# Heads normalised and gated inside the tile loop of the second attention, and the modulation chunks split two, four and two around it

## Time and profile before

| | us |
|---|---|
| median of 3 runs (1449.39 to 1458.11) | 1451.26 |
| the profiled execution | 1451.47 |
| its span, first to last instruction | 1449.6 |
| PE busy | 1267.8 (87%) |
| DVE busy | 886.1 (61%) |
| ACT busy | 599.4 (41%) |

### The profile page before, as it was taken

The page is one execution under the profiler, slowest core; times in us unless marked ns, Lnnn a source line. Parts: engine busy times, 40 slices in busy tenths (PEclk is TensorE's granted clock), DMA queues, the critical chain, the costliest instruction groups (busy, mean ns, idle before and its releaser), DMA issues.

```text
span 1449.6 us, 18593 instructions
## 1 busy us (share of the span) xinstructions
PE 1267.8 (87%) x5990; PEld 861.6 (59%) x5990; DVE 886.1 (61%) x1354; ACT 599.4 (41%) x711; POOL 162.2 (11%) x184
## 2 busy tenths in 40 slices
PE   8899999896997988579679999999999999999910
PEld 1599999653352233154257777777777777777600
DVE  0621332245325721338358888888888888888888
ACT  1332222104003011210236766767767767667601
POOL 0100000000000200000001211211211112112102
PEclk9699999996975999859879999999999999999955
DMA  8232221504430860120499999999999999999896
GB/s 344 81 121 94 68 68 34 120 8 138 137 102 16 302 170 14 66 73 1 189 340 358 381 377 367 372 374 373 381 375 367 377 372 379 380 378 374 332 315 244
DMA packets 91519, 339.20 MB, mean 234 GB/s; under 512 B 12312, under 2 KB 35880, under 8 KB 65420
## 3 DMA queue, kind: packets, MB, share of 16 engines
q1 hardware_dynamic: 75104, 301.02, 57.8%
q0 software_dynamic: 16384, 37.78, 7.5%
HBM read 317.24 MB, written 42.48 MB: 248 GB/s over the span
## 4 chain that ended last, share of the span: by engine, by line
PE 82%; DVE 9%; DMA 4%; ACT 2%; issue 1%; SPq 1%; POOL 0%; DVEq 0%; POOLq 0%; ACTq 0%
PE ps L1556 13%; PE ps L1900 12%; PE ps L1884 8%; PE ps L1880 7%; PE ps L1881 6%; PE ps L1882 6%; PE ps L1769 5%; PE ps L1866 3%; PE ps L1587 3%; PE ps L1805 3%; PE ps L1504 2%; PE ps L1744 1%; PE ps L1833 1%; PE ps L1796 1%; DMA arena<-in_w_out 1%
## 5 line engine op out<-in xcount | busy, mean ns | idle before, releaser
L1403 DVE TENSOR_TENSOR gu_lo<-w_gu,gu_hi 128x1536 fp32r<-128x1536 f32 x128 | 224.4, 1754 | 2.3 <-ACT gu_hi L965 2.3
L965 ACT ACTIVATE gu_hi<-w_gu 128x1536 fp32r<-128x1536 f32 x128 | 189.8, 1483 | 0.1
L1398 DVE TENSOR_TENSOR down_lo<-arena,down_hi 128x2048 fp32r<-128x2048 f32 x64 | 146.7, 2293 | 33.9 <-ACT down_hi L971 33.3
L1880 PE MATMUL ps<-gu_hi,xT_hi 128*112 128x512 f32 x384 | 158.2, 412 | 3.0 <-issue 2.1
L1882 PE MATMUL ps<-gu_hi,xT_lo 128*112 128x512 f32 x384 | 152.3, 397 | 0.0
L1881 PE MATMUL ps<-gu_lo,xT_hi 128*112 128x512 f32 x384 | 152.3, 397 | 0.0
L1556 PE MATMUL ps<-w_hi,hT_hi 128*128 128x300 f32 (+1 forms) x480 | 145.2, 303 | 0.7 <-DVE w_lo L1037 0.7
L1556 PE MATMUL ps<-w_lo,hT_hi 128*128 128x300 f32 (+1 forms) x480 | 144.8, 302 | 0.0
L1556 PE MATMUL ps<-w_hi,hT_lo 128*128 128x300 f32 (+1 forms) x480 | 144.7, 301 | 0.0
L971 ACT ACTIVATE down_hi<-arena 128x2048 fp32r<-128x2048 f32 x64 | 121.9, 1904 | 0.0
L1884 PE MATMUL ps<-w_gu,arena 128*112 128x512 f32 x256 | 120.2, 591 | 0.0
(11 more groups left out here) (267 smaller groups left out, 1964.2 us busy)
## 6 DMA issues: line engine op xcount, KB each, us to landing
w_gu<-in_w_exp_gate SPq DMA_DIRECT2D x64, 1024.0 KB
w_gu<-in_w_exp_up SPq DMA_DIRECT2D x64, 1024.0 KB
arena<-in_w_exp_down SPq DMA_DIRECT2D x64, 1024.0 KB, 6.1
arena<-in_w_ada SPq DMA_DIRECT2D x24, 1024.0 KB, 5.6
arena<-in_w_in SPq DMA_DIRECT2D x12, 1200.0 KB, 5.7
arena<-expert_rows SPq DMA_DIRECT2D x9, 1024.0 KB, 12.6
arena<-expert_rows SPq DMA_DIRECT2D x4, 2048.0 KB, 12.7
arena<-in_x_prompt SPq DMA_DIRECT2D x8, 512.0 KB, 10.8
```

What stands on the lines that cost most here:

```text
L965: a.activation(gu_hi[b % RING][:, :, ks], w_gu[b % U][:, :, ks], ACT.Copy).then_inc(s_ghi, 1)
L1398: v.tensor_tensor(down_lo[:, :, :], w_dn[b % RING], down_hi[:, :, :].bitcast(F32), ALU.subtract).then_inc(s_dlo, 1)
L1403: v.tensor_tensor(gu_lo[b % U][:, :, ks], w_gu[b % U][:, :, ks], gu_hi[b % RING][:, :, ks].bitcast(F32), ALU.subtract).then_inc(s_glo, 1)
L1880: pe.matmul(out, x_hi, gu_hi[r][:, :, k], start=(k == 0), stop=False)
```

## The change

- PE: chunks 0 and 1 are multiplied whole in the gate stage, between the gate logits and the wait for the log gates; chunks 2 to 5 are laid in the loop's tiles 0 to 3; chunk 6 runs between the loop and the sample states, chunk 7 behind them. The waits on `s_goe` and `s_gkve` that stood between chunks 5 and 6 now stand behind chunk 7.
- The PSUM banks of the chunks change with it.
- ACT: the ten `silu` are moved ahead of the tile loop; the two squares of each tile are moved into the loop, behind the copy of its output.
- DVE: folds 0 and 1 behind the log gates; in tile t of the loop (t from 1) fold t+1, then the sum of the squares of tile t-1, and, behind the state additions (on tile 4 between the two `qm_g` products and the sample states), the seven passes of tile t-1. Behind the loop remain the squares' sum of tile 4, folds 6 and 7, and the seven passes of tile 4.
- SP: loads 1 to 13 instead of 1 to 10 ahead of the stores; behind them loads 14 and 15 instead of 11 to 15.

```diff
-        MOD2_BANK = (2, 2, 2, 2, 2, 3, 6, 7)
+        MOD2_BANK = (6, 7, 2, 2, 2, 2, 2, 3)
...
SP
-            for i in range(1, 11):
+            for i in range(1, 14):
                 load_mod2(i)
...
-            for i in range(11, 16):
+            for i in range(14, 16):
                 load_mod2(i)
...
ACT
             for t in range(NT):
                 R = ROWS[t]
+                step(a.activation(proj[0:R, t, C_RG:C_RG + RET_W], proj[0:R, t, C_RG:C_RG + RET_W], ACT.Silu))
+                a.activation(proj[0:R, t, C_GG:C_GG + RET_W], proj[0:R, t, C_GG:C_GG + RET_W], ACT.Silu).then_inc(s_ng, 1)
+            for t in range(NT):
+                R = ROWS[t]
                 for n in range(2):
                     a.wait_ge(s_gt, 2 * t + n + 1)
...
-            for t in range(NT):
-                R = ROWS[t]
-                step(a.activation(proj[0:R, t, C_RG:C_RG + RET_W], proj[0:R, t, C_RG:C_RG + RET_W], ACT.Silu))
-                a.activation(proj[0:R, t, C_GG:C_GG + RET_W], proj[0:R, t, C_GG:C_GG + RET_W], ACT.Silu).then_inc(s_ng, 1)
-            for t in range(NT):
-                R = ROWS[t]
                 a.wait_ge(s_nq, t + 1)
                 step(a.activation(proj[0:R, t, C_RK:C_RK + RET_W], proj[0:R, t, C_RQ:C_RQ + RET_W], ACT.Square))
+                a.wait_ge(s_goe, t + 1)
                 a.activation(proj[0:R, t, C_RV:C_RV + RET_W], proj[0:R, t, C_GO:C_GO + RET_W], ACT.Square).then_inc(s_sq, 1)
...
DVE
+            for n in range(2):
+                mod_fold(n)
...
+            def head_squares(t):
+                R = ROWS[t]
+                v.wait_ge(s_sq, t + 1)
+                mark(v.tensor_reduce(head_ss[0:R, t], ...), s_nv, t + 1)
+
+            def heads(t):
+                v.wait_ge(s_small, 16 * 7)
+                v.wait_ge(s_nr, t + 1)
+                v.wait_ge(s_ng, t + 1)
...
                 if t:
-                    mod_fold(t - 1)
+                    mod_fold(t + 1)
+                    head_squares(t - 1)
...
+                    if t:
+                        heads(t - 1)
                 else:
...
+                    heads(t - 1)
                     for h in range(H):
...
-            for n in range(4, 8):
+            head_squares(PT)
+            for n in range(6, 8):
                 mod_fold(n)
+            heads(PT)
...
PE
+            for n in range(2):
+                mod_mm(n)
             pe.wait_ge(s_ls, 2)
...
                 if t < PT:
-                    pe.wait_ge(s_fold, 2 + t)
-                    mod_part(t, 0)
+                    pe.wait_ge(s_fold, 4 + t)
+                    mod_part(2 + t, 0)
...
-                        mod_part(t, 1 + c)
-                    mod_part(t, 3)
+                        mod_part(2 + t, 1 + c)
+                    mod_part(2 + t, 3)
...
+            pe.wait_ge(s_fold, 2 + 6)
+            mod_mm(6)
             for h in range(H):
...
-            pe.wait_ge(s_fold, 2 + 4)
-            mod_mm(4)
-            mod_mm(5)
+            mod_mm(7)
             pe.wait_ge(s_goe, NT)
             pe.wait_ge(s_gkve, 2 * H)
-            mod_mm(6)
-            mod_mm(7)
```

More of the change, by code:

```diff
@@ L1176, in _ @@
                 mark(v.tensor_tensor(k, k, ex[0:R, t % 2, 1], ALU.mult), s_gm, t + 1)
+            def head_squares(t):
+                R = ROWS[t]
+                v.wait_ge(s_sq, t + 1)
+                mark(v.tensor_reduce(head_ss[0:R, t], proj[0:R, t, C_RK:C_RK + 2 * RET_W].rearrange("p (h v) -> p h v", h=2 * H), AX.X, ALU.add), s_nv, t + 1)
+            def heads(t):
+                R = ROWS[t]
+                v.wait_ge(s_small, 16 * 7)
+                v.wait_ge(s_nr, t + 1)
+                v.wait_ge(s_ng, t + 1)
+                for n, (at, gate) in enumerate(((C_RQ, C_RG), (C_GO, C_GG))):
+                    o = proj[0:R, t, at:at + RET_W]
+                    o3 = o.rearrange("p (h v) -> p h v", h=H)
+                    step(v.tensor_tensor(o3, o3, head_rs[0:R, t, n * H:(n + 1) * H].unsqueeze(2).broadcast_to([R, H, DV]), ALU.mult))
+                    step(v.tensor_tensor(o, o, head_w[0:R, 2 * n], ALU.mult))
+                    if n == 0:
+                        step(v.tensor_tensor(o, o, head_w[0:R, 1], ALU.add))
+                        step(v.tensor_tensor(o, o, proj[0:R, t, gate:gate + RET_W], ALU.mult))
+                    else:
+                        mark(v.tensor_tensor(o, o, proj[0:R, t, gate:gate + RET_W], ALU.mult), s_nd, t + 1)
             step(v.memset(s_gla[:, 0], 0.0))
```

## The result

| | before | after |
|---|---|---|
| median of four runs of each, us | 1452.90 (1449.39 to 1458.11) | 1468.37 (1464.20 to 1475.66) |
| profiled execution, us | 1451.47 | 1464.20 |
| its span, us | 1449.6 | 1462.1 |
| mean granted clock | 0.909 | 0.903 |
| first gate transpose to first matmul of the output projection, us | 175.5 | 191.5 |

The ratio is 1.0109, with a 95% interval of 1.0056 to 1.0162: slower by about 1%. A second timing of the same two kernels gave 1473.12 us beside 1454.88, a ratio of 1.0127 [1.0101, 1.0152]. The predicted 1465.3 us lies 1.1 above the profiled execution and 3.1 under the first median.

A forecast was written before the change was run, and what follows sets the result against it. PE's chain was taken to bound the kernel up to the output projection, held there by chunks 4 to 7 and `w_out`. Terms summed to +25.6 through the sample states, less 11.8 in the tail: +13.8, 1465.3 us, range 1454 to 1474.

The forecast's parts named there:

- A: Gate stage: chunks 0 and 1 wait for load 1 and start cold, delaying the gate products by 13.9 us (11.6 to 15.5).
- B: Gate stage: gate products then run at full clock, leaving the lock-step of ACT and DVE: -3.4 us (0 if half clock).
- C: ACT ahead of the loop: table load and ten `silu` delay the copy that PE's scores need: +3.3 us (2.5 to 4.7).
- D: First tile of the loop: PE idles before it, so more work runs at half clock: +1.9 us (0 to 3).
- E: Loop: two squares per tile on ACT, partly covered in tiles 1 to 3, uncovered on tile 4: +2.0 us (0 to 4.8).
- F: Ahead of the sample states: chunk 6 lies in the path from a cold start: +9.4 us (7.9 to 11.5).
- G: Sample states: chunk 6 warms the clock for their first products: -1.5 us (-7.6 to 0).
- H: Tail, sample states to output projection: 24.8 us instead of 36.6, PE and `w_out` ending together: -11.8 us (-13.5 to -7).
- R2: Loop: DVE becomes the bound, PE waits on tiles 1 to 4: +6 to +8 us, 1472 us; chance 0.18.
- R1: Sample outputs and sample states: the clock stays full, 13.4 us less, 1452 us; chance 0.15, in full or in half.
- R3: Tail: PE sets it, chunk 7 and its bias at half clock: +5 us, 1470 us; chance 0.12.
- R4: Gate stage and behind the `silu`: clock full at once, A 2.3 and D 1.9 us less, 1461 us; within the forecast's 0.55.

The follow-up runs named there:

- chunk 6 behind: Kernel after the change, with chunk 6 multiplied behind the sample states, right ahead of chunk 7: 1465.06 us, ratio 1.0073 to the kernel before.
- loads 1, 2 first: Kernel after the change, with loads 1 and 2 issued ahead of the state store and the head-weight rows: 1465.91 us in a single execution.
- `w_out` ahead, heads behind: Kernel before, with chunks 0-1 in gate stage, 2-5 in loop, 6-7 behind sample states; loads 1-2 early, `w_out` before load 15 and stores, folds 6-7 earlier: 1445.22 us.

## Why the prediction was right

The sum was +13.8. S grew by 16.0 and the medians of the whole by 15.5 (1468.37 - 1452.90), so it was 2.2 us short in the stage. The mechanism was right, and the size of the loss nearly so; that the profiled execution, 1464.20, came out only 1.1 from the mark is luck, since what lies outside the stage gave back 3.5 us in this pair (last point). In the second timing the medians are 18.2 us apart. Each term, by the stage table and PE's timeline:

| term | predicted | measured | from |
|---|---|---|---|
| A, chunks 0 and 1 | +13.9 | +13.1 | first gate product 16.5, 29.6 |
| B, gate products warm | -3.4 | -2.9 | transposes at 366.48, 10.5 behind the first product at 356.01, for 13.4 |
| C, `silu` ahead of the loop | +3.3 | +3.0 | scores 8.0 behind the transposes, for 5.0 |
| D, first tile cold | +1.9 | +1.7 | 14.2 from the scores to the next transposes, for 12.5 |
| E, squares in the loop (and the clock there) | +2.0 | +3.5 | tiles 1 to 3 46.5 long, for 44.3; tile 4 to its outputs 6.1, for 4.9 |
| F, chunk 6 | +9.4 | +9.8 | 131.1 to 140.8, for none |
| G, sample states | -1.5 | -1.8 | 24.4, for 26.2 |
| H, tail | -11.8 | -10.3 | 26.3, for 36.6 |

A and B. The hole ended with the landing of load 1 (8.15 us, predicted 8.2), and half 1 took 5.05 cold for 3.5, so the cold start cost 1.5 where 2.3 was given. B came out by another path than the one summed: the prediction let tile 4's exponentials wait for DVE, but they waited for PE's products of that tile, which ended at 365.05, and the transposes at 366.48 were released by ACT. C and D are shown by moving the `silu` alone. The Trainium skill ("ScalarE: Activation LUTs", What ACT_TABLE_LOAD costs) counts a drain of about 1.4 us beside the load. No trace here shows it: the load starts at 366.35, 0.02 us behind the end of the last exponential, and the first `silu` at 367.65, 0.02 us behind the load's end; in the moved place it is 0.01.

E was the first of two terms that were too small, and what it lacked is the clock, not the squares. On tile 4 they cost 1.2, as predicted. In tiles 1 to 3, 0.25 us each had been given for squares that end just behind the cover; PE waited 0.22 us for ACT in tiles 1 and 3 and not at all in tile 2, and yet the tiles took 0.7, 1.15 and 0.45 us more. Most of that is the clock, which fell to 0.57 around 403 to 407 (the transposes of tile 2 took 1.54 us, as at half clock, for 0.87). Where it stayed up, in "chunk 6 behind" and "loads 1, 2 first", the same three tiles took 44.7 us, which with tile 4 makes E +1.7. What lets it fall in one execution and not in another stays open.

In R2 DVE was to run late. In tiles 1 to 3 DVE released no hole of PE. On tile 4 PE waited 2.37 us for DVE (L1236) ahead of the sample outputs, where it had waited 2.31 in the kernel before. The sum of the squares waited for ACT itself, here 2.73 us (timeline of DVE, kernel after):

```profile
406.19 1.22 DVE L1182 TENSOR_REDUCE head_ss<-arena 128x8 f32<-128x1024 f32 x1 [2.73 <-ACT arena L904]
```

H was the second. `w_out` left 8.0 us behind the sample states, as predicted, and took 10.2 us behind load 15's landing (10.3 predicted); but loads 14 and 15, issued behind the four stores, landed at 12.9 and 16.0 in place of 12.1 and 14.7. The step that failed by this 1.3 us is "land at about +12.1 and +14.7": it was taken from one load behind the stores, which landed in 7.0 us, where the two took 8.4 and 10.5, and half 14 and `w_out` moved with them. The recorded +24.8 is also 0.2 under its own terms (14.7 + 10.3 = 25.0).

What decided is confirmed by the edits that undo it: chunk 6 ahead of the sample states stands in the path (8 of the 8.8 us that S loses when it is moved), chunks 0 and 1 outlast the hole they fill, and in the tail only what exceeds the transfers can be won. The sentence "Moving the heads by itself wins nothing" is shown by the run with the heads only.

Rivals. R1 (the clock stays up) fell: sample outputs at 0.50, though PE was busy 15.83 of 16 us. R2 (DVE the bound) fell, above. R3 (the tail by PE) fell: chunk 7 with its bias took 10.1 us (504.41 to 514.53), where the forecast had 9.7 and R3 16.1, and `w_out` came last, by 0.75. R4 (gates cheaper) fell too: A and D were 1.0 us under their terms together, not 4.2.

Where the rest is. S grew by 16.0, the span by 12.5. The stage began 0.6 us earlier, and behind 517.79 lie 944.3 us, for 947.2 behind 502.40. The matmuls of the shared expert, which the change leaves alone, show most of it (groups of PE's instructions by line behind the output projection's start; first of the kernel before, then of the kernel after):

```profile
L1805 PE MATMUL ps<-arena 128*128 128x512 f32 (+1 forms) x80 | 36.6, 619 | 0.0
L1833 PE MATMUL ps<-arena 128*128 128x512 f32 (+1 forms) x40 | 21.5, 694 | 0.5 <-ACT arena L942 0.5
```

```profile
L1814 PE MATMUL ps<-arena 128*128 128x512 f32 (+1 forms) x80 | 35.4, 602 | 0.0
L1842 PE MATMUL ps<-arena 128*128 128x512 f32 (+1 forms) x40 | 20.0, 653 | 0.5 <-ACT arena L941 0.5
```

The same 120 records took 2.7 us less. Over the executions of this study 944.1 to 947.9 us lay behind the start, so this is their spread; in this pair it hid 2.9 us of the loss (16.0 - 0.6 - 2.9 = 12.5). The medians, 15.5 and 18.2 us apart in the two timings, don't hide it.

## What to carry over

Before work is moved off the end of an engine's queue, look whether anybody waits for that end: here DVE's heads lay under chunks and transfers in every version, and each version with them in the loop had an S at least 2.5 us longer than its twin with them behind it, part of it by the clock. Independent matmuls laid into a hole of PE win only if their weights are there when the hole opens and if they come out of a stretch that PE, not a transfer, bounds: the same split of chunks was 7.7 us worse or 6.2 us better by the place of one chunk and of two loads. Order a queue of DMAs by when each is needed, and count what lies in front of the last one: exchanging `w_out` with a load moved the wait, and won half a microsecond. Look also at what the last one waits for itself: load 15 hung on a buffer, not only on the queue.

## What the runs showed of the hardware

- Issuing one DMA can hold SP's queue for long. The first row of head weights (256 KB, spread over the partitions) took 5.29 to 5.31 us of SP in the seven traces in which it stands behind a 2 MB store, and 8.98 to 9.21 us in the five with two 1 MB loads in front as well (queue of SP, loads first):

```profile
328.25 1.02 SPq L552 DMA_DIRECT2D arena<-in_w_ada  x2
...
331.22 9.21 SPq L566 DMA_DIRECT2D arena<-in_ret_norm_w  x1
```

  So what stands behind such an instruction pays for what stands in front of it.
- Two transfers of one queue landed in the order of their issue: load 15, issued 4.2 us behind `w_out`, landed 2.5 us behind it (477.50 + 12.9 = 490.4, and 492.9; `w_out` ahead, heads behind). The Trainium skill ("DMA: Bandwidth & Descriptors", Queues, rings and completion order) says that each DMA engine takes the descriptors of a ring in order, and that a later one may still finish its write first. The order of landing here agrees with the first; the second no run here shows.
- A busy PE was no sign of a full clock. In 441 to 457, PE was busy 15.83 of 16 us with products of 64 rows and 64 columns at 0.50; in 403 to 407 it was busy throughout at 0.57, between two stretches of the loop at 1.00 (395 to 403 and 407 to 410).
- Executions differ ahead of the change too. The gate stage began at 326.3 us in the first execution of the kernel after and at 334.6 in the other, with the same code. Of these 8.3 us, 2.1 were there by 43 us, 2.0 more at the end of the input projection (266.2 and 270.3), and 4.1 came in the retention, whose matmuls ran at a mean granted clock of 0.93 in the one (276.3 to 325.4) and 0.84 in the other (280.4 to 333.6). This is as large as half of the effect, so a version is judged by its stage and by many runs, not by one total. What brings the clock down there was not tried.
